# Branch gates by seven block products instead of eight, in one layer of a hybrid decoder

## The chip, the cores and the metric

The kernel runs on one core of one Trainium2 chip. The core has engines that run beside each other and wait for each other through semaphores: TensorE (matrix products, writing to the PSUM memory), VectorE and ScalarE (elementwise work), GpSimd (nearly unused here) and SyncE, whose queue issues most transfers (DMAs). The metric is the device time of one execution in microseconds (us), as the median of several runs.

## The reference

One layer works on x, 512 tokens by 1024 features, in fp32. The part that matters here:

```
h = rmsnorm(x)
q_sb, k_sb, v_sb, q_r, k_r, v_r, g_r, gate_sb, gate_ret = split_cols(h @ w_in)
...
merged = (sigmoid(gate_sb) * (y_sb @ w_branch_sb)
          + sigmoid(gate_ret) * (y_r @ w_branch_ret))
x = x + merged @ w_out
```

`gate_sb` (gate A) and `gate_ret` (gate B) have 1024 features each and read all 1024 features of h. `y_sb` (stick-breaking attention) has 512 features, `y_r` (retention) 1024. After this come a gated feed-forward part with a short convolution and a last gated addition.

## The kernel before, in words

Features lie on the 128 partitions and tokens on the free axis, so a *feature tile* is 128 features by 512 tokens. h fills 8 such tiles. A weight *chunk* is the 8 blocks of 128 by 128 (4 where the input has 512 features) that give one output tile; chunks are numbered through the whole kernel, and `GATE0` is 36, `MERGE0` 42, `OUT0` 68.

**Split arithmetic.** Each fp32 operand is held as a high half, rounded to the format that TensorE reads, and a low half, the rest. `split3` (L455) forms a block product as high x high + high x low + low x high, three matmuls of 128 x 128 weights and 512 columns. So a chunk of 8 blocks is 24 matmuls and one of 4 blocks is 12.

**The weight ring.** A chunk goes through one of three slots `r`: SyncE loads it into `w_f[r]` (L304, once the low half of the chunk three before is done, by `s_wlo`), ScalarE casts it into `w_hi[r]` (`high`, L819, once TensorE is through with the chunk three before, by `s_used`), VectorE subtracts into `w_lo[r]` (`low`, L1302, releasing the matmuls by `s_wlo`). TensorE's `chunk` (L461) waits for `s_wlo`, runs the matmuls into one of three PSUM banks, and counts up `s_used` after its last one. The order in each engine's queue is written out by hand, and an engine takes its queue strictly in that order.

**The stage around the change.** After the fourth pair of heads come the gates of feature tiles 0 and 1 (chunks 36 to 39), branch A and branch B of tile 0 (chunks 40 and 41), and then a loop (L725) over m = 1 to 6: gate A and gate B of feature tile m + 1, then branch A (`w_a`, 4 blocks) and branch B (`w_b`, 8 blocks) of tile m. ScalarE puts the sigmoid of each gate into `fs` rows (`gate`, L1166); VectorE multiplies a branch result by its gate (`branch`, L1692, counted by `s_read`), adds the two products (`merge`, L1698), and the sum is split into high and low (`high_merged`, L1162; `low_merged`, L1704). Branches of tile 7 follow as chunks 66 and 67, then the product with `w_out` (L747).

Before the loop, the last pair's retention output is normed, gated and split (`y_norm`, `y_swish`, `high_y`, `low_y`, L1684 to L1690); chunk 41 waits for its low half. ScalarE also issues, at L1160, the load of x for the residual, 2 MB into rows 0 to 7 of `fs`.

Helpers hide the shapes in the profile: most VectorE operations have the line of `tt` (L1296), most weight casts L824 and most activations L809. What an operation is can be told by its tiles.

Of the kernel before, what the change touches and what calls it, by code (L numbers as in the profile page):

```python
# [87 lines left out]
def build(nc, xT, pT, w_in, w_a, w_b, w_out, w_up, w_down, w_pg, w_pp, g_mix, g_ffn, g_ple, g_ret, g_sbq, g_sbk,  # L88
          conv_w, conv_b, consts, decay, rope, outT):
    with ExitStack() as ctx:  # L90
# [361 lines left out]
        def _(pe):  # L452
# [261 lines left out]
            def branch_a(c, r, m):  # L714
                chunk(c, r, r, 4, T_YS)

            def branch_b(c, r, m, before=None):
                chunk(c, r, r, KD, T_YR, before=before)
# [5 lines left out]
            branch_b(GATE0 + 5, 2, 0, before={6: (s_yrlo, PAIRS)})
            with pe.Fori(0, 2) as it:  # L725
                for q in range(3):
                    c = MERGE0 + 12 * it + 4 * q
                    m = 3 * it + (q + 1)
                    pe.wait_ge(s_gate, 2 * m + 2)
                    chunk(c, (4 * q) % 3, (4 * q) % 3, KD, T_H)  # L730
                    pe.wait_ge(s_read, 2 * m - 1)
                    chunk(c + 1, (4 * q + 1) % 3, (4 * q + 1) % 3, KD, T_H)
                    pe.wait_ge(s_read, 2 * m)
                    branch_a(c + 2, (4 * q + 2) % 3, m)
                    pe.wait_ge(s_gate, 2 * m + 3)
                    branch_b(c + 3, (4 * q + 3) % 3, m)
# [70 lines left out]
        def _(act):  # L807
# [358 lines left out]
            def gate(c, q, t):  # L1166

                act.wait_ge(s_used, c + t + 1)
                run(fs[:, A_SG[(q + 2) % 3] + t, :], bank[(4 * q + t) % 3][:, :], ACT.Sigmoid, s_gate)

            with act.Fori(0, 2) as it:
                for q in range(3):
                    c = MERGE0 + 12 * it + 4 * q
                    m = 3 * it + (q + 1)

                    def two_ahead(t, kt=8):
                        high(MERGE0 // 3 + 4 * it + (4 * q + t + 2) // 3, (4 * q + t + 2) % 3, kt)

                    two_ahead(0, 4)
                    high_merged(m - 1, q)  # L1180
                    two_ahead(1)
                    gate(c, q, 0)
                    two_ahead(2)
                    gate(c, q, 1)
                    two_ahead(3)
# [108 lines left out]
        def _(dve):  # L1294
# [416 lines left out]
            with dve.Fori(0, 2) as it:
                for q in range(3):
                    c = MERGE0 + 12 * it + 4 * q
                    m = 3 * it + (q + 1)

                    def two_ahead(t, kt=8):
                        low(MERGE0 // 3 + 4 * it + (4 * q + t + 2) // 3, (4 * q + t + 2) % 3, kt)

                    two_ahead(0, 4)
                    branch(m - 1, 1, c, (4 * q + 2) % 3, q)  # L1720
                    merge(m - 1, q)
                    two_ahead(1)
                    low_merged(m - 1, q)
                    two_ahead(2)
                    two_ahead(3)
# [221 lines left out]
```

## Time and profile before

| what | value |
|---|---|
| median of 3 runs | 892.57 us (892.56 to 892.82) |
| profiled execution | 892.3 us, of which the span is 890.4 us |
| TensorE (PE) busy | 884.1 us, 99% |
| VectorE (DVE) busy | 523.0 us, 59% |
| ScalarE (ACT) busy | 411.4 us, 46% |
| GpSimd (POOL) busy | 16.5 us, 2% |
| HBM | 84.34 MB read, 97 GB/s over the span |

The span is the time from the first to the last recorded instruction of the one execution that was profiled; what lies around it is 1.9 us. Times of single instructions are counted from the start of the span. PE is the matmuls, PEld the loading of weights into TensorE, which overlaps them. Matmuls are pipelined, so their durations overlap too, and the spacing of their starts tells what each adds. "idle" with an arrow names what ended the idle time of an engine.

### The profile page before, as it was taken

How to read it: one execution, taken by the hardware profiler on the slowest of the kernel's cores; microseconds unless marked ns; L12 is line 12 of the kernel's file. 1: busy time of each engine (PE TensorE's matmuls, PEld its weight loads, DVE VectorE, ACT ScalarE, POOL GpSimd, SP SyncE). 2: the span in 40 equal slices, each digit the busy share in tenths (PEclk: the TensorE clock that was granted, in tenths of full speed). 3: DMA queues.
4: the chain of work that ended last, by engine and by line, in shares of the span. 5: the costliest groups of instructions: out<-in, count | busy, mean ns of one | idle time of the engine just before them, and what ended most of it. 6: DMA issues, size and time to landing. Idle time of an engine off the chain costs nothing.

```text
span 890.4 us, 11710 instructions
## 1 busy us (share of the span) xinstructions
PE 884.1 (99%) x4198; PEld 740.3 (83%) x4198; DVE 523.0 (59%) x660; ACT 411.4 (46%) x530; POOL 16.5 (2%) x19
## 2 busy tenths in 40 slices
PE   9999999999999999999999999999999999999998
PEld 6788898898898888888888888888888888888886
DVE  7898796796795533333556666655566643433444
ACT  7866766776775632322345333333333332323431
POOL 1500000000000000000000000000000000000000
PEclk9999999999999999999999999999999999999999
DMA  7234233233232342232323222222232323332141
GB/s 280 84 88 137 71 104 110 71 113 99 74 120 83 120 146 95 89 111 94 119 95 115 98 94 94 94 94 97 98 106 97 91 83 93 102 91 92 66 148 66
DMA packets 29819, 91.80 MB, mean 103 GB/s; under 512 B 4160, under 2 KB 5456, under 8 KB 29664
## 3 DMA queue, kind: packets, MB, share of 16 engines
q1 hardware_dynamic: 28496, 87.70, 30.5%
q10 hardware_dynamic: 1072, 3.67, 1.4%
q8 instruction: 17, 0.28, 0.1%
q0 software_dynamic: 224, 0.06, 0.1%
q14 instruction: 10, 0.08, 0.0%
HBM read 84.34 MB, written 2.10 MB: 97 GB/s over the span
## 4 chain that ended last, share of the span: by engine, by line
PE 97%; DVE 1%; DMA 1%; ACT 1%; issue 0%; SPq 0%; DVEq 0%
PE dense L457 30%; PE dense L459 30%; PE dense L458 30%; PE z L530 2%; PE aty L562 1%; DMA fs<-in_xT 1%; PE aty L458 1%; PE aty L459 1%; PE aty L457 1%; PE aty L579 1%; PE aty L577 1%; ACT fs L809 0%; DVE fs L1296 0%; DVE fs L1522 0%; PE aty L498 0%; PE aty L499 0%
## 5 line engine op out<-in xcount | busy, mean ns | idle before, releaser
L457 PE MATMUL dense<-hi,w_hi 128*128 128x512 f32 x1118 | 438.6, 392 | 0.5 <-DVE fs L1299 0.3
L458 PE MATMUL dense<-lo,w_hi 128*128 128x512 f32 x1118 | 435.6, 390 | 0.0
L459 PE MATMUL dense<-hi,w_lo 128*128 128x512 f32 x1118 | 435.5, 390 | 0.0
L1296 DVE TENSOR_TENSOR w_lo<-w_f,w_hi 128x1024 fp32r<-128x1024 f32 (+3 forms) x161 | 184.5, 1148 | 224.6 <-ACT w_hi L824 224.1
L457 PEld LDWEIGHTS dense<-hi,w_hi 128*128 128x128 f32 x1118 | 210.1, 188 | 44.5 <-DVE lo L1299 0.9
L459 PEld LDWEIGHTS dense<-hi,w_lo 128*128 128x128 f32 x1118 | 209.9, 188 | 44.1
L458 PEld LDWEIGHTS dense<-lo,w_hi 128*128 128x128 f32 x1118 | 210.1, 188 | 42.0 <-issue 0.2
L824 ACT CAST w_hi<-w_f 128x1024 fp32r<-128x1024 f32 (+2 forms) x159 | 157.3, 990 | 174.7 <-PE dense L459 172.4
L1296 DVE TENSOR_TENSOR fs<-fs 128x512 f32<-128x512 f32 (+3 forms) x115 | 86.4, 757 | 2.9 <-ACT fs L809 0.2
L809 ACT ACTIVATE fs<-fs 128x512 f32<-128x512 f32 (+2 forms) x75 | 54.4, 731 | 50.5 <-DVE fs L1299 38.6
L1296 DVE TENSOR_TENSOR lo<-fs,hi 128x512 f32 (+3 forms) x55 | 42.7, 776 | 28.8 <-ACT hi L1229 20.2
L1296 DVE TENSOR_TENSOR fs<-dense,fs 128x512 f32<-128x512 f32 x75 | 51.3, 684 | 7.4 <-PE dense L459 4.3
L1299 DVE SCALAR_TENSOR_TENSOR fs<-fs,cw 128x512 f32<-128x512 f32 x44 | 33.1, 752 | 27.9 <-ACT fs L809 24.9
L1229 ACT CAST hi<-fs 128x512 f32 (+1 forms) x22 | 13.7, 622 | 59.6 <-DVE fs L1296 59.6
L809 ACT ACTIVATE fs<-fs,cw 128x512 f32<-128x512 f32 x22 | 18.0, 816 | 43.7 <-DVE fs L1296 43.7
L457 PE MATMUL dense<-w_hi,hi 128*128 128x256 f32 x128 | 36.6, 286 | 0.0
L459 PE MATMUL dense<-w_hi,lo 128*128 128x256 f32 x128 | 36.2, 283 | 0.0
L458 PE MATMUL dense<-w_lo,hi 128*128 128x256 f32 x128 | 36.2, 283 | 0.0
L1299 DVE SCALAR_TENSOR_TENSOR lo<-fs,gain,hi 128x512 fp32r<-128x512 f32 (+1 forms) x32 | 24.4, 782 | 18.0 <-ACT hi L809 17.9
L809 ACT ACTIVATE hi<-fs,gain 128x512 fp32r<-128x512 f32 (+1 forms) x24 | 16.9, 721 | 34.4 <-DVE fs L1296 32.5
L1522 DVE TENSOR_TENSOR_SCAN fs<-z,mrev 128x511 f32<-128x511 f32 (+3 forms) x32 | 24.1, 803 | 6.6 <-ACT z L809 6.6
L1001 ACT CAST hi<-aty 128x512 fp32r<-128x512 f32 (+1 forms) x16 | 10.7, 695 | 35.1 <-PE aty L562 35.1
(131 smaller groups left out, 540.2 us busy)
## 6 DMA issues: line engine op xcount, KB each, us to landing
w_f<-in_w_in SPq DMA_DIRECT2D x52, 512.0 KB, 3.3
...
```

The lines of the kernel that those rows point to most:

```text
L457: mm(out, w1, x1, start=start, stop=False, skip_group_check=skip)
L458: mm(out, w1, x0, start=False, stop=False, skip_group_check=skip)
L459: return mm(out, w0, x1, start=False, stop=stop, skip_group_check=skip)
L530: ins = mm(out, w[:, i * P:(i + 1) * P], x[:, cols], start=(n == 0), stop=(n == 1))
L562: ins = nc.tensor.transpose(aty[:, hd, to * P:(to + 1) * P], fs[:, A_AT + hd, kb * P:(kb + 1) * P], cst[:, C_IDENT, :])
L809: return nc.scalar.activation(out, src, func, **kw).then_inc(done, 1)
L824: nc.scalar.copy(w_hi[r][:, 0:kt, :], w_f[r][:, 0:kt, :]).then_inc(s_whi, 1)
L1001: ins = nc.scalar.copy(at_blocks(hi)[:, :, to, :], aty[:, 0:2, first:first + n].rearrange("p h (b c) -> p h b c", c=P))
L1229: nc.scalar.copy(hi[:, T_G + f, :], fs[:, A_U, :]).then_inc(s_ghi, 1)
L1296: return nc.vector.tensor_tensor(out, a, b, op).then_inc(done, 1)
L1299: return nc.vector.scalar_tensor_tensor(out=out, in0=a, scalar=scalar, in1=b, op0=op0, op1=op1).then_inc(done, 1)
L1522: nc.vector.tensor_tensor_scan(fs[:, A_CP + hd, to + skip:to + width], z[:, hd, last - skip:last - width:-1], mrev[:, skip:width], 0.0, AL ...
```

## The change

The gates of feature tiles 2 to 7 are computed as a 2 by 2 block product. The rows of the weights are gate A and gate B of the tile, their two columns the input features 0 to 511 and 512 to 1023; h has the same two halves of features as its rows and two halves of the tokens (256 each) as its columns. In place of eight products of such quarters there are seven, of sums and differences of the quarters (Winograd's form of Strassen's method). Each product is 4 blocks x 3 split matmuls of 256 columns.

- *Sums of h, once:* VectorE adds high and low of each quarter (`whole`), forms four differences (`form_sum`, 1024 elements a partition each), and they are split: `high_form` on ScalarE, `low_form` on VectorE. They stand in the queues before the loop and, for form 3, in its first round. Form 3 overwrites a quarter of h.
- *Sums of the weights, for each tile:* four of 512 elements (`weight_sums` on VectorE), split by `high_weight_form` and `low_weight_form`. Two quarters are used as they are (the first from `low_first_weights`, the last from `low_last_quarter`), a third in product 3.
- *Combining:* products go to four PSUM regions; ScalarE copies two of them out (`p1_copy`, `p5_copy`), VectorE makes five additions of 256 elements into the gate rows, ScalarE applies the sigmoid.
- *Waits:* `first_forms` waits for `s_used` c, all chunks before the tile; the casts of branch B's weights and of the next tile's first chunk wait for products 5 and 7. Branch A and B now always use banks 0 and 1, and branch B of tile 7 waits for `s_read` 14.
- *Moved:* the load of x stands behind the loop on ScalarE, since its rows of `fs` hold the sums. The loops over two rounds of three tiles on TensorE, ScalarE and VectorE are written out; SyncE keeps its loop.

The core of the diff; indentation is shortened, and the old loops, which it takes out, are those printed above:

```diff
+A_S = (12, 5, 13, 6)
+A_SNAP = 7
+T_FORM = {1: 30, 2: 28, 4: 26}
...
+def quarter(t, row, col):
+  return t[:, 4 * row:4 * row + 4, col * HALF:(col + 1) * HALF]
+def h_quarter(t, row, col):
+  return quarter(t, row, col).rearrange("p (t u) n -> p t u n", u=2)
+def in_rows(tiles):
+  return tiles.rearrange("p t (u n) -> p t u n", u=2)
+def form(t, n):
+  return h_quarter(t, 0, 1) if n == 3 else in_rows(t[:, T_FORM[n]:T_FORM[n] + 2, :])
+def form_raw(n):
+  return in_rows({1: fs[:, 2:5:2, :], 2: fs[:, 8:10, :], 3: fs[:, 0:2, :], 4: fs[:, 16:18, :]}[n])
+def weight_form(n):
+  return fs[:, A_S[n - 1], :].rearrange("p (k n) -> p k n", k=4)
+def region(n):
+  return (z[:, 0, 0:HALF], z[:, 1, 0:HALF], aty[:, 0, 0:HALF], aty[:, 1, 0:HALF])[n - 1]
+def gate_half(m, t, half):
+  return fs[:, A_SG[m % 3] + t, half * HALF:(half + 1) * HALF]
...
-      ins.then_inc(s_used, 1)
+      ins.then_inc(s_used, used)
...
+def moving_h(row, col):
+  return lambda t, k: quarter(t, row, col)[:, k, :]
+def moving_form(n):
+  if n == 3:
+    return moving_h(0, 1)
+  return lambda t, k: t[:, T_FORM[n] + k // 2, (k % 2) * HALF:(k % 2 + 1) * HALF]
+def product(out, r, k0, moving, start):
+  for k in range(4):
+    ins = split3(out, w_hi[r][:, k0 + k, :], w_lo[r][:, k0 + k, :], moving(hi, k), moving(lo, k),
+          start=(start and k == 0), stop=(k == 3), skip=True)
+  ins.then_inc(s_prod, 1)
 pe.wait_ge(s_gate, 2)
 pe.wait_ge(s_yslo, PAIRS)
+branch_a(GATE0 + 4, 1, 1)
 pe.wait_ge(s_gate, 3)
+branch_b(GATE0 + 5, 2, 2, before={6: (s_yrlo, PAIRS)})
+for m in range(1, KD - 1):
+  i, c = m - 1, MERGE0 + 4 * (m - 1)
+  r1, r2, r3 = c % RING, (c + 1) % RING, (c + 2) % RING
+  pe.wait_ge(s_gate, 2 * m + 2)
+  pe.wait_ge(s_form, 5 * i + 1)
+  product(region(1), r1, 0, moving_h(0, 0), True)
+  pe.wait_ge(s_form, 5 * i + 2)
+  pe.wait_ge(s_tlo, 1)
+  product(region(2), r2, 0, moving_form(1), True)
+  pe.wait_ge(s_snap, 2 * i + 1)
+  product(region(1), r1, 4, moving_h(1, 0), False)
+  pe.wait_ge(s_form, 5 * i + 3)
+  pe.wait_ge(s_tlo, 2)
+  product(region(3), r3, 4, moving_form(2), True)
+  pe.wait_ge(s_form, 5 * i + 4)
+  pe.wait_ge(s_snap, 2 * i + 2)
+  product(region(2), r1, 0, moving_h(1, 1), False)
+  pe.wait_ge(s_wlo, c + 2)
+  pe.wait_ge(s_tlo, 3)
+  product(region(4), r2, 4, moving_form(4), True)
+  pe.wait_ge(s_form, 5 * i + 5)
+  pe.wait_ge(s_tlo, 4)
+  pe.wait_ge(s_comb, 5 * i + 1)
+  product(region(3), r2, 0, moving_form(3), False)
+  pe.wait_ge(s_read, 2 * m - 1)
+  branch_a(c + 2, r3, 0, used=3)
+  pe.wait_ge(s_read, 2 * m)
+  branch_b(c + 3, r1, 1)
 pe.wait_ge(s_gate, 16)
 pe.wait_ge(s_read, 13)
+branch_a(OUT0 - 2, 0, 0)
+pe.wait_ge(s_read, 14)
+branch_b(OUT0 - 1, 1, 1)
...
 # ScalarE
+def high_form(n, done):
+  act.wait_ge(s_tsum, done)
+  nc.scalar.copy(form(hi, n), form_raw(n)).then_inc(s_thi, 1)
+high_form(1, 1)
+act.wait_ge(s_ystat, PAIRS)
+high_form(2, 3)
-high(MERGE0 // 3, 1)
-act.wait_ge(s_yrlo, PAIRS)
-act.dma_start(fs[:, A_X:A_X + 8, :], xT).then_inc(s_xt, 16)
...
+def high_weight_form(i, n, count, r, k0):
+  act.wait_ge(s_ssum, 4 * i + count)
+  nc.scalar.copy(w_hi[r][:, k0:k0 + 4, :], weight_form(n)).then_inc(s_shi, 1)
+def high_last_quarter(c):
+  r = c % RING
+  act.wait_ge(s_wdma[r], 16 * (c // RING + 1))
+  act.wait_ge(s_used, c - 1)
+  nc.scalar.copy(w_hi[r][:, 4:8, :], w_f[r][:, 4:8, :]).then_inc(s_whi, 1)
+def high_behind(c, product, kt):
+  act.wait_ge(s_wdma[c % RING], 16 * (c // RING + 1))
+  act.wait_ge(s_prod, product)
+  nc.scalar.copy(w_hi[c % RING][:, 0:kt, :], w_f[c % RING][:, 0:kt, :]).then_inc(s_whi, 1)
+def first_forms(i, c):
+  act.wait_ge(s_used, c)
+  high_weight_form(i, 1, 1, (c + 1) % RING, 0)
+  high_last_quarter(c + 1)
+first_forms(0, MERGE0)
+high_form(4, 4)
+act.wait_ge(s_used, GATE0 + 4)
+high_form(3, 2)
+for m in range(1, KD - 1):
+  i, c = m - 1, MERGE0 + 4 * (m - 1)
+  r1, r2, r3 = c % RING, (c + 1) % RING, (c + 2) % RING
+  act.wait_ge(s_used, c)
+  high_weight_form(i, 2, 3, r3, 4)
+  act.wait_ge(s_prod, 7 * i + 1)
+  if i:
+    act.wait_ge(s_comb, 5 * i)
+  else:
+    act.wait_ge(s_tlo, 1)
+  nc.scalar.copy(p1_copy(), region(1)).then_inc(s_snap, 1)
+  high_weight_form(i, 4, 4, r1, 0)
+  high((c + 2) // RING, r3, 4)
+  high_merged(m - 1, (m - 1) % 3)
+  act.wait_ge(s_prod, 7 * i + 2)
+  nc.scalar.copy(p5_copy(), region(2)).then_inc(s_snap, 1)
+  high_weight_form(i, 3, 2, r2, 0)
+  act.wait_ge(s_prod, 7 * i + 3)
+  act.wait_ge(s_tlo, 2)
+  nc.scalar.activation(gate_half(m + 1, 0, 0), region(1), ACT.Sigmoid)
+  high_behind(c + 3, 7 * i + 5, 8)
+  act.wait_ge(s_comb, 5 * i + 2)
+  run(gate_half(m + 1, 0, 1), gate_half(m + 1, 0, 1), ACT.Sigmoid, s_gate)
+  high_behind(c + 4, 7 * i + 7, 8 if m < KD - 2 else 4)
+  act.wait_ge(s_comb, 5 * i + 5)
+  g = fs[:, A_SG[(m + 1) % 3] + 1, :]
+  run(g, g, ACT.Sigmoid, s_gate)
+  if m < KD - 2:
+    first_forms(m, c + 4)
+  else:
+    high((OUT0 - 1) // RING, (OUT0 - 1) % RING)
+act.dma_start(fs[:, A_X:A_X + 8, :], xT).then_inc(s_xt, 16)
...
 # VectorE
+def whole(rows, row, col):
+  tt(rows, h_quarter(hi, row, col), h_quarter(lo, row, col), ALU.add, s_hsum)
+def form_sum(n, a, b, h_done, t_done):
+  dve.wait_ge(s_hsum, h_done)
+  if t_done:
+    dve.wait_ge(s_tsum, t_done)
+  tt(form_raw(n), a, b, ALU.subtract, s_tsum)
+def low_form(n, done):
+  dve.wait_ge(s_thi, done)
+  tt(form(lo, n), form_raw(n), form(hi, n), ALU.subtract, s_tlo)
+dve.wait_ge(s_fac, 2 * PAIRS)
+whole(form_raw(1), 0, 0)
+whole(form_raw(3), 0, 1)
+form_sum(1, form_raw(3), form_raw(1), 2, 0)
 y_square_low(last)
+low_form(1, 1)
 low((GATE0 + 5) // 3, 2)
+whole(form_raw(2), 1, 1)
 y_low(last)
+form_sum(3, form_raw(2), form_raw(3), 3, 0)
+form_sum(2, form_raw(2), form_raw(1), 3, 2)
 y_norm(last)
 y_swish(last)
+def low_first_weights(c):
+  r = c % RING
+  dve.wait_ge(s_whi, c + 1)
+  tt(w_lo[r][:, :, :], w_f[r][:, :, :], w_hi[r][:, :, :], ALU.subtract, s_form)
+def weight_sums(i, c):
+  r1, r2 = c % RING, (c + 1) % RING
+  a11, a12 = w_f[r1][:, 0:4, :], w_f[r1][:, 4:8, :]
+  a21, a22 = w_f[r2][:, 0:4, :], w_f[r2][:, 4:8, :]
+  dve.wait_ge(s_wdma[r2], 16 * ((c + 1) // RING + 1))
+  if i:
+    dve.wait_ge(s_form, 5 * i)
+  tt(weight_form(1), a21, a22, ALU.add, s_ssum)
+  tt(weight_form(3), a11, a21, ALU.subtract, s_ssum)
+  dve.wait_ge(s_ssum, 4 * i + 1)
+  tt(weight_form(2), weight_form(1), a11, ALU.subtract, s_ssum)
+  dve.wait_ge(s_ssum, 4 * i + 3)
+  tt(weight_form(4), a12, weight_form(2), ALU.subtract, s_ssum)
+def low_weight_form(i, n, count, r, k0):
+  dve.wait_ge(s_shi, 4 * i + count)
+  tt(w_lo[r][:, k0:k0 + 4, :], weight_form(n), w_hi[r][:, k0:k0 + 4, :], ALU.subtract, s_form)
+def low_last_quarter(c):
+  r = c % RING
+  dve.wait_ge(s_whi, c + 1)
+  nc.vector.tensor_tensor(w_lo[r][:, 4:8, :], w_f[r][:, 4:8, :], w_hi[r][:, 4:8, :],
+              ALU.subtract).then_inc(s_wlo, 2)
+low_first_weights(MERGE0)
 low_y(last)
+dve.wait_ge(s_yslo, PAIRS)
+whole(form_raw(4), 1, 0)
+form_sum(4, form_raw(4), form_raw(2), 4, 3)
+weight_sums(0, MERGE0)
+low_weight_form(0, 1, 1, (MERGE0 + 1) % RING, 0)
+low_last_quarter(MERGE0 + 1)
+low_form(2, 2)
+low_form(4, 3)
-dve.wait_ge(s_sig, 1)
+dve.wait_ge(s_sig, 2)
+for m in range(1, KD - 1):
+  i, c = m - 1, MERGE0 + 4 * (m - 1)
+  r1, r2, r3 = c % RING, (c + 1) % RING, (c + 2) % RING
+  low_weight_form(i, 2, 2, r3, 4)
+  if i == 0:
+    low_form(3, 4)
+  branch(m - 1, 1, c, 2 if m == 1 else 1, (m - 1) % 3)
+  merge(m - 1, (m - 1) % 3)
+  low((c + 2) // RING, r3, 4)
+  low_merged(m - 1, (m - 1) % 3)
+  low_weight_form(i, 4, 3, r1, 0)
+  low_weight_form(i, 3, 4, r2, 0)
+  dve.wait_ge(s_prod, 7 * i + 4)
+  dve.wait_ge(s_snap, 2 * i + 1)
+  tt(gate_half(m + 1, 0, 1), region(3), p1_copy(), ALU.add, s_comb)
+  dve.wait_ge(s_prod, 7 * i + 5)
+  dve.wait_ge(s_comb, 5 * i + 1)
+  tt(gate_half(m + 1, 0, 1), region(2), gate_half(m + 1, 0, 1), ALU.add, s_comb)
+  low((c + 3) // RING, r1)
+  dve.wait_ge(s_prod, 7 * i + 7)
+  tt(gate_half(m + 1, 1, 0), region(3), p1_copy(), ALU.add, s_comb)
+  dve.wait_ge(s_snap, 2 * i + 2)
+  dve.wait_ge(s_comb, 5 * i + 3)
+  tt(gate_half(m + 1, 1, 1), gate_half(m + 1, 1, 0), p5_copy(), ALU.add, s_comb)
+  dve.wait_ge(s_comb, 5 * i + 4)
+  tt(gate_half(m + 1, 1, 0), region(4), gate_half(m + 1, 1, 0), ALU.add, s_comb)
+  if m < KD - 2:
+    low_first_weights(c + 4)
+    weight_sums(m, c + 4)
+  else:
+    low((c + 4) // RING, r2, 4)
+  if m > 1:
     dve.wait_ge(s_gate, 2 * m + 2)
+  branch(m, 0, c + 3, 0, m % 3)
+  if m < KD - 2:
+    low_weight_form(m, 1, 1, r3, 0)
+    low_last_quarter(c + 5)
+  else:
+    low((c + 5) // RING, r3)
-branch(6, 1, OUT0 - 2, 2, 0)
+branch(6, 1, OUT0 - 2, 1, 0)
```

## Rows read from the trace of the kernel before

**Rows 1.** The page: engines' busy time, share and instructions; TensorE's granted clock in tenths.

```profile
PE 884.1 (99%) x4198; PEld 740.3 (83%) x4198; DVE 523.0 (59%) x660; ACT 411.4 (46%) x530; POOL 16.5 (2%) x19
...
PEclk9999999999999999999999999999999999999999
```

**Rows 2.** The page: the chain that ended last, by engine.

```profile
PE 97%; DVE 1%; DMA 1%; ACT 1%; issue 0%; SPq 0%; DVEq 0%
```

**Rows 3.** Waits from 312 to 426 us: waiter, releaser, total us, times, longest.

```profile
DVE w_lo L1296 <- ACT w_hi L824: 73.1, 25, 3.9
ACT w_hi L824 <- PE dense L459: 66.9, 23, 4.4
ACT hi L1164 <- DVE fs L1296: 13.5, 6, 2.6
```

**Rows 4.** Windows, 306 to 420 us: busy us and instructions, clock, DMA share, GB/s.

```profile
306.00:420.00 114.00, 114.00 (x505) 94.44 (x504) 42.90 (x50) 33.34 (x44) 0.00 (x0) 1.00 0.35 118
```

**Rows 5.** Timeline of TensorE, 512 columns: start us, duration us.

```profile
300.22 0.39 PE L458 MATMUL dense<-lo,w_hi 128*128 128x512 f32 x1
...
319.94 0.39 PE L458 MATMUL dense<-lo,w_hi 128*128 128x512 f32 x1
```

**Rows 6.** Timeline of TensorE, 256 columns.

```profile
58.25 0.28 PE L457 MATMUL dense<-w_hi,hi 128*128 128x256 f32 x1
...
59.55 0.28 PE L459 MATMUL dense<-w_hi,lo 128*128 128x256 f32 x1
...
885.02 0.28 PE L457 MATMUL aty<-hi,w_hi 128*128 128x256 f32 x1
...
886.33 0.28 PE L459 MATMUL aty<-hi,w_lo 128*128 128x256 f32 x1
```

**Rows 7.** Timeline of the weight loads.

```profile
58.37 0.19 PEld L459 LDWEIGHTS dense<-w_hi,lo 128*128 128x128 f32 x1
58.48 0.19 PEld L457 LDWEIGHTS dense<-w_hi,hi 128*128 128x128 f32 x1
```

**Rows 8.** Timeline of VectorE before the loop.

```profile
302.90 1.23 DVE L1296 TENSOR_TENSOR lo<-fs,hi 128x1024 fp32r<-128x1024 f32 x1
307.15 1.23 DVE L1296 TENSOR_TENSOR w_lo<-w_f,w_hi 128x1024 fp32r<-128x1024 f32 x1 [3.03 <-ACT w_hi L824]
308.30 0.68 DVE L1296 TENSOR_TENSOR fs<-dense,fs 128x512 f32<-128x512 f32 x1
308.90 0.68 DVE L1296 TENSOR_TENSOR w_lo<-w_f,w_hi 128x512 fp32r<-128x512 f32 x1
309.50 0.68 DVE L1296 TENSOR_TENSOR fs<-dense,fs 128x512 f32<-128x512 f32 x1
310.21 0.69 DVE L1296 TENSOR_TENSOR fs<-fs 128x512 f32<-128x512 f32 x1
```

**Rows 9.** Timeline of three engines at the end of chunk 43.

```profile
316.99 0.39 PE L457 MATMUL dense<-hi,w_hi 128*128 128x512 f32 x1
317.19 1.05 ACT L824 CAST w_hi<-w_f 128x1024 fp32r<-128x1024 f32 x1 [3.90 <-PE dense L459]
318.28 1.23 DVE L1296 TENSOR_TENSOR w_lo<-w_f,w_hi 128x1024 fp32r<-128x1024 f32 x1 [3.61 <-ACT w_hi L824]
```

**Rows 10.** Groups by shape, ScalarE, 512 elements: busy us, mean ns.

```profile
L824 ACT CAST w_hi<-w_f 128x512 fp32r<-128x512 f32 x7 | 4.4, 623 | 21.8 <-PE dense L459 21.8
```

**Rows 11.** Timeline of TensorE after a wait.

```profile
10.00 0.19 PEld L457 LDWEIGHTS dense<-hi,w_hi 128*128 128x128 f32 x1 [0.63 <-DVE lo L1299]
10.00 0.51 PE L457 MATMUL dense<-hi,w_hi 128*128 128x512 f32 x1 [0.19 <-DVE lo L1299]
10.34 0.40 PE L458 MATMUL dense<-lo,w_hi 128*128 128x512 f32 x1
```

**Rows 12.** Transfers of x: KB each, median us to landing.

```profile
fs<-in_xT ACTq DMA_DIRECT2D x1, 2048.0 KB, 10.7
```

**Rows 13.** Groups by shape, TensorE, the warm-up.

```profile
L639 PE MATMUL aty<-hi 128*128 128x512 f32 x18 | 6.8, 556 | 1.5 <-DVE hi L1309 1.5
```

More of the change, by code:

```diff
@@ L76 @@
 A_P = 14
+A_S = (12, 5, 13, 6)
+A_SNAP = 7
+HALF = SEQ // 2
+T_FORM = {1: 30, 2: 28, 4: 26}
 N_F32 = 18
@@ L153, in build @@
         s_read = sem("s_read")
+        s_hsum, s_tsum, s_thi, s_tlo = sem("s_hsum"), sem("s_tsum"), sem("s_thi"), sem("s_tlo")
+        s_ssum, s_shi, s_form = sem("s_ssum"), sem("s_shi"), sem("s_form")
+        s_prod, s_snap, s_comb = sem("s_prod"), sem("s_snap"), sem("s_comb")
         s_xt, s_rsq, s_rehi, s_relo, s_acc = sem("s_xt"), sem("s_rsq"), sem("s_rehi"), sem("s_relo"), sem("s_acc")
@@ L289, in v_turned, with p1_copy, p5_copy @@
             return misc.rearrange("p (b h d) -> p b h d", b=NT, h=2)[:, :, hd, :]
+        def quarter(t, row, col):
[10 more added lines that the diff above has]
+            return fs[:, A_S[n - 1], :].rearrange("p (k n) -> p k n", k=4)
+        def p1_copy():
+            return fs[:, A_SNAP, 0:HALF]
+        def p5_copy():
+            return fs[:, A_SNAP, HALF:SEQ]
+        def region(n):
+            return (z[:, 0, 0:HALF], z[:, 1, 0:HALF], aty[:, 0, 0:HALF], aty[:, 1, 0:HALF])[n - 1]
+        def gate_half(m, t, half):
+            return fs[:, A_SG[m % 3] + t, half * HALF:(half + 1) * HALF]
         def yq(t):
@@ L459, in split3, with chunk @@
                 return mm(out, w0, x1, start=False, stop=stop, skip_group_check=skip)
-            def chunk(c, r, b, kt, tile0, hooks=None, k_first=0, last=True, before=None, halved=False):
+            def chunk(c, r, b, kt, tile0, hooks=None, k_first=0, last=True, before=None, halved=False, used=1):
                 if halved:
@@ L712, in _, with branch_a, branch_b @@
             chunk(GATE0 + 3, 0, 0, KD, T_H, {5: lambda: stat_y(last)})
[L714 to L718, printed above, removed]
+            def branch_a(c, r, b, **kw):
+                chunk(c, r, b, 4, T_YS, **kw)
+            def branch_b(c, r, b, before=None):
+                chunk(c, r, b, KD, T_YR, before=before)
+            def moving_h(row, col):
+                return lambda t, k: quarter(t, row, col)[:, k, :]
@@ L720, in _ @@
             pe.wait_ge(s_gate, 2)
             pe.wait_ge(s_yslo, PAIRS)
-            branch_a(GATE0 + 4, 1, 0)
+            branch_a(GATE0 + 4, 1, 1)
             pe.wait_ge(s_gate, 3)
[L724 to L736, printed above, removed]
+            branch_b(GATE0 + 5, 2, 2, before={6: (s_yrlo, PAIRS)})
@@ L1164, in high_merged @@
                 nc.scalar.copy(hi[:, T_M + m, :], fs[:, A_SG[ring], :]).then_inc(s_mhi, 1)
[L1166 to L1185, printed above, removed]
+            def high_weight_form(i, n, count, r, k0):
+                act.wait_ge(s_ssum, 4 * i + count)
+                nc.scalar.copy(w_hi[r][:, k0:k0 + 4, :], weight_form(n)).then_inc(s_shi, 1)
@@ L1706, in low_merged @@
                 tt(lo[:, T_M + m, :], fs[:, A_SG[ring], :], hi[:, T_M + m, :], ALU.subtract, s_mlo)
-            low(MERGE0 // 3, 1)
-            dve.wait_ge(s_sig, 1)
+            dve.wait_ge(s_sig, 2)
             branch(0, 0, GATE0 + 5, 1, 0)
[L1711 to L1725, printed above, removed]
-                    dve.wait_ge(s_gate, 2 * m + 2)
-                    branch(m, 0, c + 3, (4 * q + 2) % 3, (q + 1) % 3)
+            for m in range(1, KD - 1):
[30 more added lines that the diff above has]
+                if m > 1:
+                    dve.wait_ge(s_gate, 2 * m + 2)
+                branch(m, 0, c + 3, 0, m % 3)
[4 more added lines that the diff above has]
+                    low((c + 5) // RING, r3)
```

3 lines of the change are left out of this document (removed).

## The prediction

> **What bounds the kernel now.** I read the page's totals first: TensorE busy 99% of the span, at full clock all through, VectorE 59%, ScalarE 46% [rows 1]. Then the chain that ended last: 97% of it is TensorE [rows 2]. A kernel in this condition gets faster only by giving TensorE less to do, and gets slower by any wait that reaches TensorE. Then the waits of the stretch that the change rewrites: VectorE waits for ScalarE, ScalarE for TensorE, and no line has TensorE waiting [rows 3]. Last its windows: 114 us, all 114 busy, 505 matmuls begun [rows 4]. That is six feature tiles of 84 matmuls (24 gate A, 24 gate B, 12 branch A, 24 branch B).
>
> Matmul durations overlap (390 ns each), so the price of one is the spacing of starts. 512 columns: from 300.22 to 319.94 us lie 87 matmuls, 226.7 ns each [rows 5]. A tile takes 84 x 0.2267 = 19.04 us.
>
> **The change, part by part.**
>
> *TensorE work.* Per tile, 48 matmuls of 512 columns become 84 of 256 (7 products x 4 blocks x 3 split terms). 256-column matmuls start 11 apart in 1.30 us at 58 us and in 1.31 us at 885 us: 118.2 to 119.1 ns, I take 118.7 [rows 6]. The weight loads, recorded at 190 ns each, follow each other just as closely, 110 to 120 ns [rows 7], so they overlap and are no bound. 48 x 0.2267 = 10.88 us becomes 84 x 0.1187 = 9.97 us (a product 1.42): 0.91 us less a tile, **-5.5 us** for six. That is half of what one eighth of the arithmetic suggests, because two half-width matmuls cost 237 ns against 227.
>
> The Trainium skill (TensorE: Matmul & The Clock Gate, section "Back-to-back issue gap") gives N/2.4 + 2.5 ns at full clock: 215.8 and 109.2 ns. By it, as an estimate, a tile would save 1.19 us and the six 7.1. The rows are higher at both widths, and the sum goes by the rows.
>
> *Times I use for the rest.* VectorE, start to start: a 1024-element operation 1.15 us, a 512-element one 0.60; a result used by the next operation of the same engine costs 0.11 more; a 512 result is there after 0.69 [rows 8]. Matmul group end to ScalarE start about 0.20 after the next group's first start; ScalarE end to VectorE start 0.04, which I take for every hand-over between engines; the 1024 cast lasts 1.05 [rows 9] and a 512 cast 0.62 [rows 10]. When TensorE has run dry, its second matmul comes 0.34 instead of 0.23 us after the first: 0.11 lost on reloading [rows 11], 0.15 with the hand-over. None of the new operations exists before, but all are adds, subtracts and casts of these sizes.
>
> *First rewritten tile (tile m=1, from 306.12 us: the matmul at 316.99 us [rows 9] opens branch A, 48 matmuls later).* VectorE gets four `whole`, four `form_sum`, four `low_form` of 1024 elements, 13.8 us, on top of what it had. Those up to `low_y(last)` fit into its idle time before 304 us: `low_y` ends near 304.1 as now [rows 8], and branch B of tile 0 starts on time. From there on VectorE is never idle and everything TensorE needs is behind something. `whole(4)`, `form_sum(4)` to 306.5; four weight sums to 309.0; low of form 1 done 309.8. Product 2 was due at 306.12 + 1.42 = 307.54 and starts at 309.9: **2.4 us** dry. Then last quarter, `low_form(2)`, `low_form(4)`, `branch(0,0)`, low of form 2: 0.6 + 0.6 + 1.15 + 1.15 + 0.6 + 0.69 from 309.1, done 313.9; product 4, due 312.8, starts 314.0: **1.2**. Then `low_form(3)`, branch, merge, low of w_a, low_merged (it waits for ScalarE's cast), low of form 4, done 318.3; product 5, due 315.45, starts 318.5: **3.0**. Sum **+6.7 us**.
>
> The bounds of this term: from below 4, if ScalarE and VectorE hand over faster and `whole` overlaps more; from above 8.5, at 3% more for each VectorE operation and 0.06 us for each hand-over.
>
> *Tiles 3 to 7 (m=2 to 6).* The forms of h are ready, and sums of weights are made in VectorE's free time late in the tile before. But `first_forms` on ScalarE waits for `s_used` c, the end of branch B, so the high half of weight form 1 starts only when product 1 does. From t = 0 (start of product 1): cast 0.20 to 0.82, low of form 1 0.86 to 1.54, product 2 at 1.69 with reloading, due 1.42: 0.27 dry. Behind it on VectorE stand last quarter, form 2, branch, merge, low of w_a, low_merged, form 4: 0.86 + 0.6 x 3 + 0.72 + 0.6 + 0.8 + 0.6 + 0.69 = 6.05. Product 5 starts at 6.2, due 5.96: 0.24. After that nothing is late: form 3 by 6.7 for 9.1; branch B's weights (cast only after product 5) by 10.2 for 13.2; the next tile's first weights and sums by 16.3 of 18.6. A tile is 6.2 + 3 x 1.42 + 36 x 0.2267 = 18.63 against 19.04. So 0.51 of the 0.91 goes back, **+2.6 us** for five tiles. From below 0.2 a tile, from above 0.75 with the slower hand-overs.
>
> *Behind the loop.* Branch B of tile 7 now waits for `s_read` 14 (it was 13), the read of branch B of tile 6, whose bank it takes. That read stands behind the cast of `OUT0` (0.20 to 1.25) and its low half (to 2.44): done 3.2 us after branch B ended, while branch A fills 2.72: **+0.55 us**.
>
> *At nothing.* The load of x (2 MB, 10.7 us to landing [rows 12]) moves on ScalarE's queue from 304 us to about 420 us, since its rows hold sums until then; it lands near 431, and the first residual needs it after output tile 0, near 438. If the weight loads beside it made it 7 us slower, it would show. SP's loads change in one way: three of four in a tile are released by VectorE 2 to 4 us after product 1 and needed 5 us or more later. The two-iteration loops become straight code.
>
> **Sum**, against the profiled execution (892.3 us, span 890.4): -5.5 + 6.7 + 2.6 + 0.55 = **+4.3 us**, 896.6. The median shown is 0.27 above that execution: **896.9 us**. Everything behind stays as dense as before.
>
> **Rivals.**
> 1. *TensorE's clock falls in the first tile.* It runs 1.4, 2.8, 1.4 us of matmuls between gaps of 2.4, 1.2 and 3.0. For: the 18 warm-up matmuls took 6.8 us where 18 x 0.227 = 4.1 are due, so TensorE at the start of the kernel, idle before, was below full speed [rows 13]. Against: no gap of this length comes later in the trace, so it shows neither. Price as in that row, 2.7 us once: 899.6. The same skill page (section "Why this matters for your kernels") warns that idle gaps between bursts of matmuls put the clock back to its lower level; that is this case.
> 2. *Not slower: the first tile is not late.* The total is -2.35 us plus the stall of the first tile, so that stall decides. At 0 the time is 890.2; up to 2.3 us it is not slower; up to 4.1 it can't be told from no change. For it: ScalarE and VectorE are half idle on the page. Against: it needs VectorE to get through 20 operations after 304 us about 4 us sooner, and their durations vary by hundredths.
> 3. *Half-width matmuls cost more with fresh weights each time.* If each took as long as a weight load is recorded, 190 ns, a tile gains 84 x 0.07 = 6 us and the time is 933. Rows 6 and 7 speak against it; both already have new weights for each matmul.
> 4. *Steady tiles run later:* the chain of eight VectorE operations at 0.06 more each, or instruction supply of straight code: 0.5 us a tile, 899.4.
>
> **Chances.** Forecast 0.62 (own range 895.2 to 898.6), clock 0.14, not late 0.12 (half of it faster), half-width 0.02, steady later 0.10. What a measurement here can tell from no change is 0.2%, 1.8 us: slower 0.84, same 0.10, faster 0.06. Range 893.8 to 900.5.
>
> **What would show it.** In the changed trace: 256-column starts 118 to 119 ns apart; TensorE waits of some 2.4, 1.2 and 3.0 us at products 2, 4 and 5 of the first tile, each released by VectorE's subtraction into w_lo; then a tile every 18.6 us with two waits of a quarter microsecond; one of half a microsecond before branch B of tile 7; full clock in all slices. It is wrong if the first tile has less than 4 us of waits, or if tiles 3 to 7 take 18.1 or over 19.1 us each.

## The result, and the profile after

The changed kernel takes 899.14 us, median of six runs (897.53 to 899.76), against 892.57 (892.22 to 892.82) before: ratio 1.0072, 95% interval 1.0059 to 1.0085. It is slower by 6.6 us; 896.9 was forecast, range 893.8 to 900.5. The measured time lies in that range, but outside the forecast's own range of 895.2 to 898.6. Runs of the changed kernel lie at two levels about 1.5 us apart (here one of six at the lower, two of four in a later set), so kernels are compared below level with level.

The page of the changed kernel, first its busy line, then the chain that ended last, to be read against [rows 1, 2]:

```profile
PE 883.4 (98%) x4414; PEld 748.1 (83%) x4414; DVE 574.4 (64%) x750; ACT 428.9 (48%) x576; POOL 16.6 (2%) x19
...
PE 93%; DVE 3%; ACT 2%; DMA 1%; issue 0%; SPq 0%; DVEq 0%; ACTq 0%
```

216 more matmuls (six tiles, 36 more in each), VectorE 51 us busier, and the chain has 6% of VectorE, ScalarE and DMA in it where it had 3%. The page's clock line shows 9 in all slices, as before; it is too coarse for what follows. TensorE's waits from 304 to 440 us, where it had none [rows 3]:

```profile
PE z L502 <- DVE w_lo L1419: 5.0, 2, 2.7
PE aty L502 <- DVE w_lo L1419: 0.9, 1, 0.9
PE dense L502 <- DVE fs L1419: 0.3, 1, 0.3
```

Its timeline (start us, duration us): products 1, 2, 4 and 5 of the first rewritten tile, the start of the second tile, and branch B of tile 7.

```profile
306.25 0.28 PE L502 MATMUL z<-hi,w_hi 128*128 128x256 f32 x1
...
310.10 0.39 PE L502 MATMUL z<-hi,w_hi 128*128 128x256 f32 x1 [2.26 <-DVE w_lo L1419]
...
314.17 0.39 PE L502 MATMUL aty<-hi,w_hi 128*128 128x256 f32 x1 [0.94 <-DVE w_lo L1419]
...
318.61 0.39 PE L502 MATMUL z<-hi,w_hi 128*128 128x256 f32 x1 [2.75 <-DVE w_lo L1419]
...
332.71 0.28 PE L502 MATMUL z<-hi,w_hi 128*128 128x256 f32 x1
...
429.51 0.50 PE L502 MATMUL dense<-hi,w_hi 128*128 128x512 f32 x1 [0.34 <-DVE fs L1419]
```

The first tile takes 332.71 - 306.25 = 26.46 us, where it had 19.04. The same stretch as windows, against [rows 4]:

```profile
306.00:319.00 13.00, 7.05 (x53) 6.38 (x52) 12.85 (x18) 8.08 (x14) 0.00 (x0) 1.00 0.27 89
319.00:323.00 4.00, 4.00 (x24) 4.00 (x23) 1.63 (x4) 1.36 (x2) 0.00 (x0) 0.57 0.29 109
323.00:440.00 117.00, 116.63 (x709) 103.74 (x708) 78.27 (x122) 45.21 (x78) 0.00 (x0) 1.00 0.34 119
```

In the first, VectorE is busy 12.85 of 13 us and TensorE 7.05. In the second TensorE is busy all the time, but at a granted clock of 0.57, so mostly at 1.2 GHz, its lower level: 24 matmuls begin in 4 us, where 33 do at full clock. The timeline of that window, three starts:

```profile
319.07 0.34 PE L502 MATMUL z<-hi,w_hi 128*128 128x256 f32 x1
...
320.28 0.41 PE L502 MATMUL z<-hi,w_hi 128*128 128x256 f32 x1
320.49 0.41 PE L503 MATMUL z<-lo,w_hi 128*128 128x256 f32 x1
...
322.61 0.28 PE L504 MATMUL aty<-hi,w_lo 128*128 128x256 f32 x1
```

Starts are 0.21 us apart in place of 0.12. The 17 intervals from 319.07 to 322.61 take 3.54 us where 17 x 0.12 = 2.04 are due: 1.5 us lost.

**Balance of the 6.6 us between the spans (890.4 and 897.0).** Start of the first tile +0.1; first tile +7.4; tiles 3 to 7 together -1.6 (they start 18.71 us apart from 332.71 on, where it was 19.04); branch B of tile 7 +0.6. That is 6.5; the rest is rounding. What lies around the span grew from 1.9 to 2.2 us.

### The profile page after: what moved, and what is told of

Read it like the earlier page. It is cut to its first block, busy times and chain, and to the rows that moved or that the text cites. A ratio compares the mean times of both kernels' runs of the same rounds, so it can differ in the third digit from the quotient of the medians.

```text
span 897.0 us, 12241 instructions
## 1 busy us (share of the span) xinstructions
PE 883.4 (98%) x4414; PEld 748.1 (83%) x4414; DVE 574.4 (64%) x750; ACT 428.9 (48%) x576; POOL 16.6 (2%) x19
## 4 chain that ended last, share of the span: by engine, by line
PE 93%; DVE 3%; ACT 2%; DMA 1%; issue 0%; SPq 0%; DVEq 0%; ACTq 0%
PE dense L502 27%; PE dense L504 26%; PE dense L503 26%; PE z L575 2%; DVE fs L1419 2%; PE aty L503 2%; PE aty L504 2%; PE aty L502 2%; PE z L502 1%; PE z L503 1%; PE z L504 1%; PE aty L607 1%; DMA fs<-in_xT 1%; DVE w_lo L1419 1%; PE aty L624 1%; ACT fs L886 1%
## 5 line engine op out<-in xcount | busy, mean ns | idle before, releaser
L502 PE MATMUL dense<-hi,w_hi 128*128 128x512 f32 x1022 | 401.1, 393 | 1.8 <-DVE lo L1422 1.1
L503 PE MATMUL dense<-lo,w_hi 128*128 128x512 f32 x1022 | 398.1, 390 | 0.0
L504 PE MATMUL dense<-hi,w_lo 128*128 128x512 f32 x1022 | 398.0, 389 | 0.0
L1419 DVE TENSOR_TENSOR w_lo<-w_f,w_hi 128x1024 fp32r<-128x1024 f32 (+2 forms) x155 | 176.6, 1141 | 157.8 <-ACT w_hi L901 153.1
L502 PEld LDWEIGHTS dense<-hi,w_hi 128*128 128x128 f32 x1022 | 191.9, 188 | 42.3 <-issue 2.1
L504 PEld LDWEIGHTS dense<-hi,w_lo 128*128 128x128 f32 x1022 | 191.8, 188 | 40.4
L503 PEld LDWEIGHTS dense<-lo,w_hi 128*128 128x128 f32 x1022 | 192.0, 188 | 38.1 <-issue 0.2
L901 ACT CAST w_hi<-w_f 128x1024 fp32r<-128x1024 f32 (+2 forms) x141 | 138.5, 982 | 113.5 <-PE dense L504 111.2
L502 PE MATMUL z<-hi,w_hi 128*128 128x256 f32 x96 | 28.7, 298 | 5.0 <-DVE w_lo L1419 5.0
L1252 ACT CAST w_hi<-fs 128x512 fp32r<-128x512 f32 x24 | 14.9, 620 | 30.6 <-PE dense L504 30.5
```

What stands on the lines that cost most here:

```text
L502: mm(out, w1, x1, start=start, stop=False, skip_group_check=skip)
L503: mm(out, w1, x0, start=False, stop=False, skip_group_check=skip)
L504: return mm(out, w0, x1, start=False, stop=stop, skip_group_check=skip)
L901: nc.scalar.copy(w_hi[r][:, 0:kt, :], w_f[r][:, 0:kt, :]).then_inc(s_whi, 1)
L1252: nc.scalar.copy(w_hi[r][:, k0:k0 + 4, :], weight_form(n)).then_inc(s_shi, 1)
L1419: return nc.vector.tensor_tensor(out, a, b, op).then_inc(done, 1)
```

## The experiments

Each is an edit of the changed kernel, with its core shown; "..." marks what is left out. The runs fall into three sets, each on one chip of its own: e1 to e4; e0 and e5 to e7; e8 and e9. The kernel before took 892.09, 892.13 and 892.17 us in them, so times of different sets can be compared to about 0.1 us.

**The changed kernel again (e0_changed).**

> The changed kernel once more, so that the others of this call are compared with it on one chip. Its tiles and waits as in its first profile, 6.2 to 7 us above the kernel before; 1.6 us of that where the clock is at half for one stretch, more if for two.

897.96 us (897.15 to 898.70), ratio 1.0063 (1.0046 to 1.0079): two runs at 897.2, two at 898.7. This is the reference for the levels below.

**Forms of the weights cast one chunk earlier (e1_early_forms).**

```
-                act.wait_ge(s_used, c - 1)
+                act.wait_ge(s_used, c - 2)
                 nc.scalar.copy(w_hi[r][:, 4:8, :], w_f[r][:, 4:8, :]).then_inc(s_whi, 1)
...
-                act.wait_ge(s_used, c)
+                act.wait_ge(s_used, c - 1)
                 high_weight_form(i, 1, 1, (c + 1) % RING, 0)
```

> The cast of weight form 1 and of the last quarter waits for the end of branch A (s_used c - 1) instead of branch B. Theory (in tiles 3 to 7 the two short TensorE waits come from this cast starting only with product 1): both waits vanish in tiles 3 to 7, a tile takes 84 x 0.120 + 36 x 0.227 = 18.2 us instead of 18.7, in all 2.5 us less than the changed kernel: about 896.6 us. Rival (VectorE's amount of work is the bound there, whenever it starts): the waits stay and the time stays at 899.1.

895.07 us (894.94 to 896.48), ratio 1.0035 (1.0022 to 1.0048); level by level 2.2 less than e0 (four runs at 895.0, two at 896.5), where 2.5 was expected. The cast of form 1 in tile 4, first in the changed kernel (where the tile starts at 351.43 us), then here (350.60), each with VectorE's low half behind it:

```profile
351.63 0.62 ACT L1252 CAST w_hi<-fs 128x512 fp32r<-128x512 f32 x1 [6.11 <-PE dense L504]
...
352.28 0.69 DVE L1419 TENSOR_TENSOR w_lo<-fs,w_hi 128x512 fp32r<-128x512 f32 x1 [3.16 <-ACT w_hi L1252]
```

```profile
345.84 0.62 ACT L1252 CAST w_hi<-fs 128x512 fp32r<-128x512 f32 x1 [1.16 <-DVE fs L1419]
...
348.20 0.68 DVE L1419 TENSOR_TENSOR w_lo<-fs,w_hi 128x512 fp32r<-128x512 f32 x1
```

Form 1 is now ready 1.7 us before its tile begins, where it came 1.5 us into it. Tiles 3 to 7 take 18.26 us each in place of 18.71, and their short waits are gone. So 0.45 us a tile was the condition on which ScalarE's two casts waited, not a lack of VectorE or ScalarE time. The first tile's three waits stayed (2.25, 0.93, 2.74).

**Spare matmuls in the first tile's gaps (e2_spare_matmuls).** Before the three waits TensorE multiplies ones into an unused bank, 6, 2 and 8 times.

```
+                if i == 0:
+                    spare(6)
                 pe.wait_ge(s_form, 5 * i + 2)
```

> 16 spare matmuls of 512 columns (6, 2 and 8) stand ahead of the waits before products 2, 4 and 5 of the first rewritten tile, with no other use; nothing else changes. Theory (the clock falls because TensorE idles in that tile, and that costs 1.6 us beside the waits): full clock in all windows behind 304 us, the three products start where they did, 1.6 us less than the changed kernel: about 897.5 us. Rival (the stretch at half clock is hidden behind VectorE, or falls with another cause): 899.1 or, if the spare matmuls delay the products, more.

897.37 us (897.26 to 897.55), ratio 1.0059 (1.0042 to 1.0076). Its windows:

```profile
306.00:319.00 13.00, 10.77 (x70) 9.01 (x70) 12.84 (x19) 7.88 (x14) 0.00 (x0) 1.00 0.29 107
319.00:323.00 4.00, 4.00 (x35) 4.00 (x34) 1.94 (x3) 1.37 (x2) 0.00 (x0) 1.00 0.14 50
```

The needed products started as long after the start of the tile as in the changed kernel, within 0.1 us, so VectorE paced them as before; but the clock stayed at 1.00, 35 matmuls begin in the second window, not 24, and the first tile takes 24.96 us, not 26.46. All of the 1.5 us lies behind the start of product 5: from there to the next tile are 12.61 us, where the changed kernel and e0 have 14.10. That is the price of the clock in the two profiled runs, both of the upper level. The four runs lie within 0.3 us of each other, 1.3 us under e0's upper level and 0.2 over its lower one, so the spare matmuls gain nothing against a run of the lower level. The traces of e4 suggest why (below).

**Another order of the first tile's work (e3_order).** Same operations. VectorE takes what the seven products need first, and branches A and B of tile 0, their merge and the low halves for branch A of tile 1 after it; ScalarE's casts of that tile are put in the same order.

```
                 low_weight_form(i, 2, 2, r3, 4)
...
                 if i == 0:
+                    low_weight_form(i, 4, 3, r1, 0)
+                    low_last_quarter(c + 1)
+                    low_form(4, 3)
+                    low_weight_form(i, 3, 4, r2, 0)
                     low_form(3, 4)
+                    first_sum()
+                    dve.wait_ge(s_sig, 2)
+                    branch(0, 0, GATE0 + 5, 1, 0)
                 branch(m - 1, 1, c, 2 if m == 1 else 1, (m - 1) % 3)
```

> Same work in the first rewritten tile in another order on VectorE and ScalarE: forms of the weights and low_form(2) first, then last quarter, low_form(4), form 3, low_form(3), and only then branch A and B of tile 0, merge, the weights of branch A. Theory (the waits of products 4 and 5 are an order matter, that of product 2 is the backlog before the loop): the wait before product 2 stays at 2.3 us, those before products 4 and 5 (0.9 and 2.8 us idle) vanish, the clock stays full; 5.8 us less than the changed kernel: about 893.3 us. Rival (the backlog of VectorE must be paid in that tile in whatever order): later products or the branches wait instead, about 899.

894.51 us (893.16 to 894.67), ratio 1.0024 (1.0014 to 1.0033). TensorE's timeline has one wait of the three left, and the clock's windows show that this one is enough:

```profile
309.68 0.39 PE L502 MATMUL z<-hi,w_hi 128*128 128x256 f32 x1 [2.25 <-DVE w_lo L1427]
```

```profile
306.00:311.00 5.00, 2.75 (x22) 2.54 (x22) 4.97 (x8) 4.34 (x8) 0.00 (x0) 0.97 0.00 0
311.00:314.00 3.00, 3.00 (x16) 3.00 (x16) 3.00 (x5) 2.10 (x4) 0.00 (x0) 0.50 0.16 19
```

The first tile takes 22.27 us, 4.2 less than 26.46: the waits of products 4 and 5 (1.2 and 3.0 with reloading). The expectation counted another 1.6 for a clock that would stay up after a single wait of 2.3 us. It fell to 0.50, in eight of ten runs by their times: the other two lie 1.3 us below, with a mean clock of 0.999 where the eight have 0.997 to 0.998.

**Another bank for branch B of tile 6 (e4_bank).**

```
-                branch_b(c + 3, r1, 1)
+                branch_b(c + 3, r1, 2 if m == KD - 2 else 1)
...
-            pe.wait_ge(s_read, 14)
             branch_b(OUT0 - 1, 1, 1)
```

> Branch B of tile 6 goes to bank 2, so that branch B of tile 7 needs s_read 13 only. Theory: the wait of 0.6 us before branch B of tile 7 vanishes, 898.5 us. Rival: the wait moves to output tile 0, 899.1.

897.87 us (896.62 to 897.95), ratio 1.006 (1.0043 to 1.0077). The wait before branch B of tile 7 is gone, and both levels lie 0.6 to 0.8 us under e0's. In its profiled run the clock was down twice in the first tile, after the waits of products 2 and 5:

```profile
312.00:314.00 2.00, 2.00 (x11) 2.00 (x11) 2.00 (x4) 0.06 (x1) 0.00 (x0) 0.50 1.01 397
...
318.00:320.00 2.00, 1.79 (x8) 1.80 (x9) 1.09 (x3) 0.00 (x0) 0.00 (x0) 0.50 0.70 248
```

That is not twice the cost, as the expectation of e0 had it ("more if for two"): product 3 ran at half clock while VectorE prepared product 4, and the wait for product 4 disappeared in exchange. Product 5 begins 12.35 us after the start of the tile, in e0, with one fall, 12.36: the first fall costs nothing. That gives a reading of the two levels. The three upper runs have a mean clock of 0.996 (two falls), the lower run 0.998 (one); in e0, e1 and e7 both levels have the same mean clock, 0.997 to 0.998, so one fall each. If the one fall comes after the wait for product 5, it costs 1.5 us; if after the wait for product 2, nothing. All this fits, but no trace of a run at the lower level was kept, so it isn't shown.

**The three edits together (e5_three)**: the order of e3, the early casts of e1, the bank of e4.

> The three changes together: order of the first tile, early cast of form 1, bank 2 for branch B of tile 6. Theory (they act in different places and add up): only the wait of 2.3 us before product 2 of the first tile is left; tiles 3 to 7 take 18.26 us each, 3.9 less in all than before; first tile 18.3 + 2.4. In sum 2.2 us below the kernel before, plus 1.6 where the clock falls after that one wait, as it did with the order alone: 0.4 to 0.8 us below it. Rival (they share the same slack of VectorE): some wait comes back in tiles 3 to 7 and the kernel is slower than before.

890.34 us (890.10 to 891.85), ratio 0.9984 (0.9974 to 0.9993): now faster than before, by 1.8 us, as the theory had it (2.2 where the clock stays up, 0.4 to 0.8 where it falls). Only the 2.25 us before product 2 is left, and tiles follow each other every 18.26 us. Seven of ten runs lie at 890.1 to 890.4 with a mean clock of 1.000, three at 891.6 to 891.9 with 0.997 to 0.998. What stands before product 2 in the queues, the cast of form 1 on ScalarE first:

```profile
307.31 0.62 ACT L1251 CAST w_hi<-fs 128x512 fp32r<-128x512 f32 x1
```

```profile
304.14 1.22 DVE L1426 TENSOR_TENSOR fs<-hi,lo 128x1024 f32<-128x1024 f32 x1
305.39 1.22 DVE L1426 TENSOR_TENSOR fs<-fs 128x1024 f32<-128x1024 f32 x1
...
308.46 0.69 DVE L1426 TENSOR_TENSOR fs<-w_f,fs 128x512 f32<-128x512 f32 x1
309.07 0.69 DVE L1426 TENSOR_TENSOR w_lo<-fs,w_hi 128x512 fp32r<-128x512 f32 x1
```

The high half is there at 307.93, but the low half that product 2 waits for begins at 309.07, behind the weight sums of three other forms. The two operations from 304.14 make form 4 of h, which only product 6 needs. So some of this wait is order too: an estimate from these rows is up to 1.1 us of 2.4. No run tried it.

**The h sums on GpSimd (e6_gpsimd).** GpSimd is idle [rows 1]; e5 with five of VectorE's eight 1024-element sums given to it.

```
+            pool_tt(form_raw(2), h_quarter(hi, 1, 1), h_quarter(lo, 1, 1), ALU.add, s_hsum)
...
-            whole(form_raw(2), 1, 1)
...
-            form_sum(2, form_raw(2), form_raw(1), 3, 2)
```

> As the kernel of three changes, and five of the eight sums of h (1024 elements each) go from VectorE to GpSimd. Theory (the wait before product 2 is VectorE's backlog of whole(4), form_sum(4) and the weight sums): GpSimd takes about 3.2 us for each, twice its 1.59 us for 512 elements, all are done by 305 us; the wait before product 2 falls from 2.3 to about 0.7 us, too short for the clock to fall; 4.0 us below the kernel before. Rival (GpSimd and VectorE get in each other's way where VectorE reads two operands from SBUF): VectorE's operations from 289 to 305 us become longer than 1.23 us, chunk 41 or product 2 waits for it, no gain over the three changes or a loss.

894.97 us (894.86 to 895.03), ratio 1.0032 (1.0019 to 1.0045): 4.6 us worse than e5. Its timeline, VectorE alone, then GpSimd and VectorE beside each other ("x2" is two operations in a row):

```profile
288.78 1.22 DVE L1443 TENSOR_TENSOR fs<-fs 128x1024 f32<-128x1024 f32 x1
...
290.18 2.41 POOL L496 TENSOR_TENSOR fs<-hi,lo 128x1024 f32<-128x1024 f32 x1 [248.22 <-DVE fs L1443]
290.60 6.41 DVE L1443 TENSOR_TENSOR lo<-fs,hi 128x1024 fp32r<-128x1024 f32 x2 [0.59 <-ACT hi L1048]
292.66 6.57 POOL L496 TENSOR_TENSOR fs<-fs 128x1024 f32<-128x1024 f32 x2
296.93 3.38 DVE L1443 TENSOR_TENSOR w_lo<-w_f,w_hi 128x1024 fp32r<-128x1024 f32 x1
...
301.02 0.47 PE L519 MATMUL dense<-hi,w_hi 128*128 128x512 f32 x1 [3.21 <-issue]
```

VectorE's operation goes from 1.22 to 3.2 to 3.4 us while GpSimd's takes 2.4 to 3.3: one seems to wait for the other. What was handed over cost more than it freed, and TensorE waited 3.21 us before 301.02 in a place where it had not (the row names no releaser; a low half of VectorE's ended at 300.92), with the clock at 0.57 from 302 to 306 us. With a further 0.41 us of idle time before 310.08, the first tile begins at 311.59, 5.6 us later than in e5. Within it the theory was half right: it takes 19.74 us in place of 20.89, and product 2 waits 1.13 us, now for ScalarE's cast of form 1 and not for VectorE's queue:

```profile
313.57 0.69 DVE L1443 TENSOR_TENSOR w_lo<-fs,w_hi 128x512 fp32r<-128x512 f32 x1 [1.01 <-ACT w_hi L1268]
```

```profile
314.32 0.39 PE L519 MATMUL z<-hi,w_hi 128*128 128x256 f32 x1 [1.13 <-DVE w_lo L1443]
```

5.6 - 1.2 = 4.4 us, against 4.5 between the spans. The Trainium skill (GPSIMD Engine Reference, section "1. Specifications") says that GpSimd shares its memory interfaces with VectorE and contends with VectorE instructions of two SBUF inputs; all of these have two SBUF inputs, and the trace agrees: they took 2.6 to 2.8 times as long.

**Form 4 ahead of the branch (e7_form4_first).**

```
+                if i:
+                    low_weight_form(i, 4, 3, r1, 0)
                 branch(m - 1, 1, c, 2 if m == 1 else 1, (m - 1) % 3)
```

> The changed kernel with the low half of weight form 4 ahead of branch, merge, weights of branch A and low_merged on VectorE in tiles 3 to 7. Theory (product 5 waits at the end of that chain of eight operations, product 2 for form 1 alone): the wait before product 5 vanishes, that before product 2 stays, 0.23 us less a tile, 1.1 us less than the changed kernel. Rival (both waits come from the late cast together): the wait at product 5 moves to product 6 or 7, no change.

896.35 us (896.21 to 897.86), ratio 1.0047 (1.003 to 1.0064); level by level 0.8 to 0.9 less than e0, where 1.1 was expected. Tiles 3 to 7 take 18.52 us: the wait before product 5 (0.2 us a tile) goes, that before product 2 stays. With e1 it splits the 0.45 us a tile into the two waits of the forecast.

**Seven products from tile 3 on only (e8_five_tiles).** Tile 2's gates stay eight block products, and the first forms are made beside them. With the early casts and the bank, not the new order.

```
-            for m in range(1, KD - 1):
-                i, c = m - 1, MERGE0 + 4 * (m - 1)
+            chunk(MERGE0, 0, 0, KD, T_H)
...
+            for m in range(2, KD - 1):
+                i, c = m - 2, MERGE0 + 4 * (m - 1)
```

> Seven products for feature tiles 3 to 7 only; the gates of tile 2 stay as in the kernel before, and VectorE and ScalarE prepare the sums of h and of the first weights beside them. The early cast of form 1 and bank 2 for branch B of tile 6 are in it too. Theory (the first rewritten tile loses only because its sums come too late): TensorE waits nowhere from 300 to 440 us, the clock stays full; 19.04 us for tile 2, 18.26 for each of five others, 3.9 us below the kernel before, about 888.2 us. Rival (the sums only move their place and the wait with them): a wait of 1 to 2 us appears before the branches of tile 1 or product 4 of the next tile, no better than the kernel of three changes, 890.3.

888.19 us (887.99 to 888.25), ratio 0.9954 (0.9941 to 0.9968): the best, 4.0 us under before and 2.2 under e5 (1.8 of it in the span, 886.4 against 888.2; e9, which is e5 with spare matmuls, took 890.36 in the same set as e8), though it saves in one tile less. TensorE waits for nothing between 304 and 445 us:

```profile
304.00:320.00 16.00, 16.00 (x72) 13.26 (x71) 12.23 (x15) 10.18 (x12) 0.00 (x0) 1.00 0.37 115
320.00:440.00 120.00, 120.00 (x728) 107.95 (x727) 81.45 (x125) 49.14 (x82) 0.00 (x0) 1.00 0.36 123
```

```profile
325.01 0.28 PE L502 MATMUL z<-hi,w_hi 128*128 128x256 f32 x1
...
343.27 0.28 PE L502 MATMUL z<-hi,w_hi 128*128 128x256 f32 x1
```

Where VectorE was busy 12.85 of 13 us, it is now busy 12.23 of 16. One tile's saving of 0.8 us was given up, and the stall before product 2 went: tile 2 takes 19.04 us (305.97 to 325.01) where e5's takes 20.89, and that is the 1.8 us between the spans.

**e5 with eight spare matmuls before product 2 (e9_three_spare).**

> The kernel of three changes with 8 spare matmuls of 512 columns in its one wait (2.3 us) before product 2 of the first tile. Theory (its runs near 891.8 us against 890.2 are those in which the clock fell after that wait): all runs lie at 890.2 us within 0.3, none at 891.8. Rival: the two levels stay.

890.36 us (890.31 to 890.50), ratio 0.9979 (0.997 to 0.9989), ten runs, none at e5's upper level. Its window from the first product on:

```profile
306.00:311.00 5.00, 4.59 (x31) 3.91 (x30) 4.96 (x8) 4.34 (x8) 0.00 (x0) 1.00 0.00 0
```

e5's lower level (890.1 to 890.4) and this kernel agree within 0.2 us, on two chips. So e5's two levels are the clock, which falls or doesn't fall after the same wait.

## Why the prediction came out as it did

The sum was +4.3 us against a measured +6.6 between the spans. Step by step:

- **The matmuls.** A tile of e1 or e5, where nothing waits, takes 18.26 us against 18.13 forecast and 19.04 before: 0.78 saved in place of 0.91. That is 18.26 - 36 x 0.2267 = 10.10 us for 84 matmuls of 256 columns, 120 ns each where 118.7 were forecast. Right within 0.13 us a tile. The rates of the Trainium skill (TensorE: Matmul & The Clock Gate, section "Back-to-back issue gap") put a tile, as an estimate, at 19.04 - 1.19 = 17.85; the trace doesn't agree, with 18.26.
- **The first tile's waits.** Product 2 began 2.4 us behind its due time (forecast 2.4), product 4 another 1.2 (1.2), product 5 another 3.0 (3.0), each released by a subtraction into w_lo. Right, as a sum over VectorE's queue in order (the three add up to 6.6, which the prediction wrote as 6.7). e3, the same work in another order, removed the second and third; so what they cost was the order. What the first is made of is only in part known (e5, e6).
- **Full clock in all slices.** This is the step that failed, a term that the sum put at nothing: 1.5 us in the first tile, shown by the window at 0.57 and taken away by e2. The forecast named it as its first rival with 0.14, at a price of 2.7 us from the warm-up; its mechanism happened beside the forecast's sum, at 1.5. The error was in the chance. "No gap of this length comes later" in the trace before was read as evidence against, though it says only that nothing was known; a clock that was low after the idle start was the one row there was [rows 13]. The price was too high since one half-clock stretch of 17 half-width matmuls was lost, not 18 of full width. By the total alone, 899.14 lies nearer to the fourth rival (899.4, steady tiles later) than to this one (899.6); only the trace tells them apart. With 1.5 added, the forecast's sum is 5.8; the rest is 0.1 at the start, 0.1 in the first tile and 0.08 in each of the other five. The rule of the Trainium skill that stood with this rival (same page, section "Why this matters for your kernels"), that idle gaps between bursts put the clock back, agrees with the traces in part: the clock fell after idle times of 2.75 us (the changed kernel) and 2.25 us (e3, e4), but in the changed kernel, e1 and e5 it stayed at 1.00 after a first wait of 2.25 us too.
- **Tiles 3 to 7.** 18.63 us forecast, 18.71 measured, with waits of 0.2 us before products 2 and 5; e1 and e7 took them away together and singly. The cause named, ScalarE's wait for the end of branch B, was right: moving it by one chunk gave 2.2 us.
- **Branch B of tile 7.** 0.55 forecast, 0.6 measured, 0.6 to 0.8 by e4.
- **At nothing.** The load of x, now issued at 421.13 us, landed after 8.4 us and nothing waited for it. Right.
- **The rival on the other side** (the first tile isn't late) was wrong for this kernel; e8 shows its condition. It put the point of decision at 2.3 us of stall; e5 has about 2.4 there and is faster only through the 2.2 of e1 and the 0.6 of e4.

What stays open: what decides whether the clock falls after the same wait, since runs of one kernel (e3, e5) differ in it; whether the lower level of the changed kernel (its one run at 897.53 has the same mean clock as the others) is a fall after the wait for product 2 in place of that for product 5, as e4 suggests; and how much of the wait before product 2 another order would take away. So e8 is the best kernel found here, and it isn't shown that tile 2 must stay as it was.
